# Heads of the first two layers taken two at a time in six visits of a group, and the modulation tiles of both layers dealt out anew

## What is computed

```python
def hybrid_layer(x, c, cos, sin, pre_g, post_g, w_ada, b_ada, w_in, w_out):
    mod = jnp.einsum('bd,de->be', jax.nn.silu(c), w_ada) + b_ada
    shift, scale, gate = jnp.split(mod, 3, axis=-1)
    h = rms_norm(x, pre_g) * (1 + scale[:, None, :]) + shift[:, None, :]
    proj = jnp.einsum('bsd,de->bse', h, w_in)
    qa, ka, va, ga, qb, kb, vb, gb = jnp.split(proj, SPLIT_POINTS, axis=-1)
    ...
    o_a = merge(dilated_mixture_attention(qa, ka, heads(va, N_HEADS_A))) * jax.nn.silu(ga)
    o_b = merge(moba_attention(qb, kb, heads(vb, N_HEADS_B))) * jax.nn.silu(gb)
    y = jnp.einsum('bse,ed->bsd', jnp.concatenate([o_a, o_b], axis=-1), w_out)
    y = rms_norm(y, post_g)
    return x + gate[:, None, :] * y
...
mod = (silu_c @ w_mod[l] + b_mod[l]).reshape(B, 3 * N_SUB, 1, D)
h = rms_norm_2(x, norm_g[l, 1]) * (1.0 + sc) + sh
```

## Time and profile before

| | |
|---|---|
| runs | 1634.32 to 1634.64 us, median 1634.32 us |
| profiled execution | 1635.31 us, of which the span is 1633.5 us |
| granted TensorE clock | 0.999 of full speed |
| busy | PE 98%, DVE 72%, ACT 47%, POOL 4% |

### The profile page before, as it was taken

One profiled execution on the slowest core, in us unless ns is written; L12 is line 12 of the kernel. 1 busy time (PEld: TensorE's weight loads), 2 busy tenths in 40 slices (PEclk: granted clock), 3 DMA queues, 4 the chain that ended last, 5 costly groups with the idle time before them and its releaser, 6 DMA issues.

```text
span 1633.5 us, 20618 instructions
## 1 busy us (share of the span) xinstructions
PE 1607.6 (98%) x7958; PEld 1325.4 (81%) x7958; DVE 1173.3 (72%) x1921; ACT 774.3 (47%) x1221; POOL 63.0 (4%) x95
## 2 busy tenths in 40 slices
PE   6999999999999999999999999999999999999998
PEld 5778777888888888887776888888888888888886
DVE  7778898748976666477645789867877758666654
ACT  4766565542221223254445555535554563554552
POOL 0000100010000000020001100001000100010000
PEclk9999999999999999999999999999999999999999
DMA  9866676325666665242122387866777585455551
GB/s 378 334 246 232 259 269 210 130 99 195 219 217 215 222 226 199 90 160 77 65 88 84 135 329 290 316 232 259 258 282 273 181 329 214 163 192 192 182 183 37
DMA packets 93187, 337.49 MB, mean 207 GB/s; under 512 B 10641, under 2 KB 11281, under 8 KB 92833
## 3 DMA queue, kind: packets, MB, share of 16 engines
q1 hardware_dynamic: 90848, 328.11, 56.1%
q0 software_dynamic: 2240, 8.06, 1.5%
HBM read 335.08 MB, written 1.05 MB: 206 GB/s over the span
## 4 chain that ended last, share of the span: by engine, by line
PE 54%; DVE 2%; issue 1%; ACT 0%; POOL 0%; DVEq 0%; POOLq 0%; ACTq 0%
PE bank L292 52%; PE bank L295 2%; DVE sb_tm L301 0%; DVE sb_XN L309 0%; ACT sb_arena L298 0%; ACT sb_XN L298 0%; DVE sb_X L301 0%; DVE sb_XN L301 0%; DVE sb_sg L316 0%; DVE sb_arena L319 0%; DVE sb_XC L301 0%; DVE sb_w8r L301 0%; DVE sb_w5r L301 0%; POOL sb_rstd L301 0%; DVE sb_arena L312 0%
## 5 line engine op out<-in xcount | busy, mean ns | idle before, releaser
L298 ACT ACTIVATE sb_hi<-sb_w 128x1024 fp32r<-128x1024 f32 x428 | 431.4, 1052 | 289.1 <-DMA sb_w<-in_w 242.3
L292 PE MATMUL bank<-sb_hT,sb_hi 128*128 128x512 f32 x1600 | 527.6, 394 | 0.0
L292 PE MATMUL bank<-sb_hi,sb_hT 128*128 128x512 f32 x1280 | 418.6, 398 | 3.8 <-ACT sb_hT L298 3.3
L292 PEld LDWEIGHTS bank<-sb_hT,sb_hi 128*128 128x128 f32 x1600 | 292.3, 188 | 58.4
L292 PEld LDWEIGHTS bank<-sb_hi,sb_hT 128*128 128x128 f32 x1280 | 241.2, 189 | 60.4 <-issue 7.7
L312 DVE CUSTOM_DVE_ANT_0 sb_w<-sb_w,sb_cb 128x1024 f32<-128x1024 f32 x144 | 174.7, 1218 | 0.0
L301 DVE TENSOR_TENSOR sb_sg<-bank,sb_sg 128x512 f32<-128x512 f32 (+1 forms) x90 | 58.9, 660 | 102.5 <-ACT sb_sg L298 80.7
L298 ACT ACTIVATE sb_sg<-bank 128x512 f32<-128x512 f32 (+1 forms) x98 | 54.9, 574 | 126.5 <-PE bank L292 122.7
L298 ACT ACTIVATE sb_arena<-bank 128x512 f32<-128x512 f32 (+1 forms) x108 | 58.2, 561 | 74.4 <-PE bank L295 38.8
L292 PE MATMUL bank<-sb_arena 128*128 128x64 f32 (+5 forms) x400 | 87.7, 345 | 0.5 <-DVE sb_arena L319 0.5
L301 DVE TENSOR_TENSOR sb_tm<-bank,sb_rows 128x512 f32<-128x512 f32 x40 | 27.6, 691 | 72.4 <-PE bank L292 69.6
(11 more groups left out here) (470 smaller groups left out, 3204.3 us busy)
## 6 DMA issues: line engine op xcount, KB each, us to landing
sb_w<-in_w SPq DMA_DIRECT2D x428, 512.0 KB, 4.2
sb_w<-in_mw SPq DMA_DIRECT2D x192, 512.0 KB, 4.6
sb_rows<-in_na_rpb POOLq DMA_DIRECT2D x16, 96.0 KB, 2.3
sb_X<-in_x SPq DMA_DIRECT2D x1, 1024.0 KB, 4.9
sb_cb<-in_cvec POOLq DMA_DIRECT2D x2, 512.0 KB, 6.9
sb_XC<-in_ctx POOLq DMA_DIRECT2D x1, 1024.0 KB, 9.7
sb_arena<-in_sg_ln_g POOLq DMA_DIRECT2D x1, 1024.0 KB, 6.2
sb_arena<-in_sg_ln_b POOLq DMA_DIRECT2D x1, 1024.0 KB, 9.5
```

Of the source, the lines that this page charges most:

```text
L292: return self.e.matmul(out, a, b, start=start, stop=stop)
L298: return self.e.activation(out, a, f, **kw)
```

## The change

Three edits. (1) A group is worked on in six visits v = 0 to 5 in place of eleven. Visit v of PE holds, in this order: the transposes of head 2v-2, the value products of heads 2v-4 and 2v-3, the scores of heads 2v and 2v+1, the transposes of head 2v-1. ACT copies and exponentiates in turn for both heads, DVE masks both heads, and divides in visits 3 and 5. The visits of group A now stand after units 15, 17, 19, 21, 23, 24 of layer 1 and 10, 12, 14, 16, 18, 19 of layer 2; those of B after 24, 26, 28, 30, 32, 33 and 22, 24, 26, 28, 30, 31. (2) Of the 48 modulation tiles 16 to 63, thirty instead of twenty-four are worked on after units 16 to 34, and eighteen between units 43 and 70 instead of twenty-four between 40 and 66. (3) The squares of the context rows on ACT stand after units 4 to 7 of layer 2 instead of 11 to 14.

```diff
-    for first, last, count in ((16, 34, 24), (40, 66, 24), (W_F00 + 8, W_MX - 10, 64), (W_F01 + 4, W_F10 - 10, 32),
+    for first, last, count in ((16, 34, 30), (43, 70, 18), (W_F00 + 8, W_MX - 10, 64), (W_F01 + 4, W_F10 - 10, 32),
...
-        for i in range(11):
-            B1[0].setdefault(15 + i, []).append(("A", i))
-            B1[0].setdefault(23 + i, []).insert(i < 3, ("B", i))
-            B1[1].setdefault(10 + i, []).append(("A", i))
-            B1[1].setdefault(22 + i, []).insert(0, ("B", i))
+        for v in range(6):
+            B1[0].setdefault((15, 17, 19, 21, 23, 24)[v], []).append(("A", v))
+            B1[0].setdefault((24, 26, 28, 30, 32, 33)[v], []).insert(v == 0, ("B", v))
+            B1[1].setdefault((10, 12, 14, 16, 18, 19)[v], []).append(("A", v))
+            B1[1].setdefault((22, 24, 26, 28, 30, 31)[v], []).insert(0, ("B", v))
...
+        def pe_attention(e, l, g, v):
+            if 1 <= v <= 4:
+                pe_turn(e, l, g, 2 * v - 2)
+            if v >= 2:
+                pe_weigh(e, l, g, 2 * v - 4)
+                pe_weigh(e, l, g, 2 * v - 3)
+            if v < 4:
+                pe_score(e, l, g, 2 * v)
+                pe_score(e, l, g, 2 * v + 1)
+            if 1 <= v <= 4:
+                pe_turn(e, l, g, 2 * v - 1)
...
+        def act_attention(e, l, g, v):
+            for x in range(2):
+                if 1 <= v <= 4:
+                    act_weights(e, l, g, 2 * v - 2 + x)
+                if v < 4:
+                    act_exp(e, l, g, 2 * v + x)
...
+        def dve_attention(e, l, g, v):
+            if v < 4:
+                dve_scores(e, l, g, 2 * v)
+                dve_scores(e, l, g, 2 * v + 1)
+            if v in (3, 5):
+                dve_weighed(e, l, g, v // 4)
...
-                if 11 <= u < 15 and l == 1:
-                    square(e, "cx0", XC, u % 2, (u - 11) // 2, SQ, [done(LD["xc"], 0), *rows_turned("a1")])
+                if 4 <= u < 8 and l == 1:
+                    square(e, "cx0", XC, u % 2, (u - 4) // 2, SQ, [done(LD["xc"], 0), *rows_turned("a1")])
```

More of the change, by code:

```diff
@@ new lines, in pe_score @@
+        def pe_score(e, l, g, h):
+            pr, po = h // 2, 64 * (h % 2)
+            b = BANK["S", l, g, h] = HB3.take()
+            for f in b.free() + heads_ready(l, g, "q") + heads_ready(l, g, "k"):
+                e.wait_ge(*f)
+            q, k = qT[g], kT[g]
+            e.mm(b.ap[:, 0:128], q[po:po + 64, pr, 0:128], k[po:po + 64, pr, 0:128], True, True)
+            e.mm(b.ap[:, 128:384], q[po:po + 64, pr, 128:256], k[po:po + 64, pr, :], True, True).then_inc(
+                SCO.sem, SCO.put(l, g, h))
+            b.till = ((SMX, l, g, h),)
@@ new lines, in pe_turn, with pe_weigh @@
+        def pe_turn(e, l, g, h):
+            b = BANK["P", l, g, h] = HB3.take()
+            for f in b.free():
+                e.wait_ge(*f)
+            e.wait_ge(*done(EX, l, g, h))
+            for x in range(3):
+                m = e.tr(b.ap[:, x * 128:(x + 1) * 128], PB[h % 3][:, x * 128:(x + 1) * 128], ident)
+            m.then_inc(TRP.sem, TRP.put("P", l, g, h))
+            b.till = ((AE, "PT", l, g, h),)
+        def pe_weigh(e, l, g, h):
+            b = bank[7]
+            if h % 4 == 0:
@@ L1008, in pe_attention @@
                 for f in b.free():
                     e.wait_ge(*f)
[L1010 to L1046, removed]
@@ new lines, in pe_weigh @@
+            e.wait_ge(*done(AE, "PT", l, g, h))
+            for j in range(2):
+                e.wait_ge(*done(AE, "p", l, "v", g, j))
+            v, pt, c, o = vv[g], PT[h % 3], slice(h * 64, h * 64 + 64), h % 4 * 64
+            e.mm(b.ap[:, o:o + 64], pt[:, 0:128], v[:, 0, c], True, True)
+            e.mm(b.ap[:, 256 + o:320 + o], pt[:, 128:256], v[:, 0, c], True, False)
+            e.mm(b.ap[:, 256 + o:320 + o], pt[:, 256:384], v[:, 1, c], False, True).then_inc(PVS.sem, PVS.put(l, g, h))
@@ new lines, in pe_weigh, with act_weights @@
+            b.till = ((DE, "O", l, g, h // 4),)
+        def act_attention(e, l, g, v):
[4 more added lines that the diff above has]
+                    act_exp(e, l, g, 2 * v + x)
+        def act_weights(e, l, g, h):
+            e.wait_ge(*done(TRP, "P", l, g, h))
+            if h >= 3:
+                e.wait_ge(*done(PVS, l, g, h - 3))
+            elif g:
+                e.wait_ge(*done(PVS, l, 0, (6, 7, 5)[h]))
+            e.act(PT[h % 3], BANK["P", l, g, h].ap[:, 0:384], ACT.Copy).then_inc(AE.sem, AE.put("PT", l, g, h))
@@ new lines, in dve_weighed @@
+        def dve_weighed(e, l, g, q):
+            r = stat[:, l, g, q * 4:q * 4 + 4, 2:4]
+            e.wait_ge(*done(EX, l, g, q * 4 + 3))
+            e.recip(r, r).then_inc(DE.sem, DE.put("recip", l, g, q))
+            e.wait_ge(DE, DE.n)
+            e.wait_ge(*done(PVS, l, g, q * 4 + 3))
+            if l:
+                for f in squares_done("cx0"):
+                    e.wait_ge(*f)
+            c = slice(g * 512 + q * 256, g * 512 + q * 256 + 256)
+            e.tt(y[:, :, c].rearrange("p j (h d) -> p j h d", d=64),
+                 bank[7].ap[:, :].rearrange("p (j h d) -> p j h d", j=2, h=4),
+                 r.rearrange("p h j -> p j h").unsqueeze(3).to_broadcast([128, 2, 4, 64]), ALU.mult).then_inc(
+                     DE.sem, DE.put("O", l, g, q))
```

61 lines of the change are left out of this document (19 added, 42 removed).

## The result

The changed kernel takes 1619.9 us (median of 4 runs, 1619.5 to 1620.3), the kernel before 1634.5 (4 runs, 1634.3 to 1634.6): a ratio of 0.991, 95% interval 0.9898 to 0.9921, or 14.6 us less. The forecast was 6.3 us less, and the range ended at 1624.0. Direction and place were right, the size was not. (The profiled execution of the kernel before was 0.8 us above its median, so the spans of the two profiles differ by more, 15.4 us.)

The account below looks back on a forecast made before the run. PE, busy 1607.6 of 1633.5 us, was taken as the bound; 6.0 + 0.4 + 0.2 - 0.3 = 6.3 us less gave 1629.0 profiled, 1628.0 as median, range 1624.0 to 1631.5.

Parts of the forecast that it names:

- the price of the second score head: PE's double visits: the odd head's scores cost 0.11 + 0.11 + 0.22 + 0.22 us instead of 0.85; 6.0 us saved.
- Price (c): PE's score pairs: the odd head also overlaps the even head's last 256-column instruction; 13.7 us a group, 9.4 saved.
- The three prices: PE's score pairs: array drains every head, drain saved, or last instruction also overlapped; 3.0, 6.0 or 9.4 us saved.
- rival 1: PE's score pairs: heads overlap in the array at price (c); 9.7 us less, 1624.6 us; chance 0.30.
- price (b): PE's score pairs: no row change or unhidden load between two 64-row heads; 14.6 us a group, 6.0 saved; chance 0.40.
- Tiles in layer 1: Six more modulation tiles on DVE, units 16 to 34: a late tile delays the y transposes 0.3 us, bounds 0 and 2.
- DVE's cover: Last division of group B, layer 1: DVE comes 0.5 us late against a cover of 0.94, so no cost.
- The waits at 198 and 159.86 us: PE's waits in early layer 2 and late layer 1 go with the new tile times: 0.4 and 0.2 us gained.
- Squares: Context-row squares, four at some 0.8 us, moved into ACT's waits at 188 to 200 us of layer 2: cost nothing.
- Rival 3: Visits 1 to 3: three-bank ring makes the last transposes wait for ACT's copy; 4.5 us slower, 1638.8; chance 0.05.
- The lead persists: After layer 2 the same units start earlier by the same amount up to the end, else the forecast fails.

Follow-up runs that it names:

- same rows: The changed kernel with heads taken in the order 0, 2, 1, 3, 4, 6, 5, 7, so both of a pair lie in the same 64 rows: 1627.7 us.
- unstalled run: The changed kernel with the Silu of the condition rows in unit 14, not 20, and layer 2's first y transposes in unit 30, not 29: 1626.1 us.
- paired neighbourhood attention: The changed kernel with the neighbourhood attention's scores of an even and an odd head also issued next to each other: 1618.4 us.
- scores issued ahead: The paired neighbourhood attention with each pair of scores issued at the end of the odd item before, except items 12 and 13: 1620.6 us.
- old tiles: The changed kernel with the modulation tiles at their old times (24 and 24), pairs and moved squares kept: 1622.0 us.

## Why the prediction failed, point by point

- **The step that failed is the price of the second score head.** "The second head costs 0.11 + 0.11 + 0.22 + 0.22 instead of 0.85" is exactly what it costs in the same 64 rows (same rows: 0.65, a full visit 4.06). In the other 64 rows it costs 0.01 (a full visit 3.41). Price (c) let only the even head's last instruction overlap, since I thought of the overlap as something between neighbours in the queue; in fact the two chains of four run side by side. The three prices left out the one that held, 0.01, though the rule of rival 1 leads to it if every instruction is given its partner. 16 pairs x 0.64 = 10.3 us is the missing term. The rest of the forecast stood: in the same rows, where price (b) is paid, the changed kernel is 6.8 us faster than the kernel before, where 6.3 was forecast.
- **The rule of the Trainium skill** that matmuls in different row groups run at the same time ("TensorE: Matmul & The Clock Gate", Part 3, Packing small matmuls) is what the trace now shows, at 13 ns from start to start where it gives about 4 (7 ns at 512 columns); I gave the rule 0.30 and priced it at a third of what it does, and "By that, (c) holds" was my misreading: if every instruction runs beside its partner, the whole odd head goes. The argument against it (float32 scores take two instructions with a load each) counted for nothing.
- **Tiles in layer 1**, +0.3 us ahead of the `y` transposes: right in place and size (0.2, at 147 us), as was DVE's cover. Alone, in eleven visits, the wait can be 1.25 us, inside the bounds of 0 and 2, and for the reason given: the tile of unit 32 lands late.
- **The waits at 198 and 159.86 us** (0.4 and 0.2) are gone as forecast with the pairs; in eleven visits the same tile times removed them too, and other waits cost more. With the pairs the tile times are worth 2.1 us, not 0.6: the stretch of 185 to 205 us was read as it was, and not as it would be once PE comes to it 8 us earlier, where DVE is the late one at 221 us. Squares: nothing, right within the 0.36 us of one wait.
- **Rival 3** (the ring of three banks) was real but small: two of twelve places, 0.45 and 0.49 us, each with ACT late (at 93 us behind 2.0 us of Silu, at 122 behind a table load of 1.28 and a rounding). New waits came to 2.3 us, where 0.3 was taken. Against the ledger: 17.3 us less on PE (7.0 that also come in same rows, 10.3 by the overlap), 2.3 of new waits, 0.6 of old ones gone, so 15.6 over the two layers; unit 80 starts 15.5 us earlier, and the span fell by 15.4. Of the 7.0, 6.0 were forecast; the full visit agrees to 0.01 us, so the missing 1.0 lies in the other visits, and which of them was not traced.
- **The lead persists**: the unit starts are 15.4 to 15.6 us earlier from layer 2's end to the last one, as written.

## What to carry to other kernels

Where a kernel has matmuls of 64 rows, look for a partner in the other 64 rows and issue the two next to each other: in float32 the second was free here, at 128, 256 and 512 columns, and that was 10.3 us of PE's stream. Then count what the followers need: the exponential, the copy and the bank have the same time as before but half the distance on PE, and an engine that takes its work in order must have the piece that PE needs next ahead of the piece that waits for PE. When a price is bounded by the nearest rows, ask what mechanism would make it zero, and keep zero in the range if no row excludes it.

## What was not expected of the hardware

- Two float32 chains in the two halves of the rows run entirely beside each other: starts 13 ns apart for each of four instructions, 0.86 us for both against 0.85 for one; at 512 columns 1.05 us for both against 2.1 for two. In the same half they take 0.65 us more, with no change of rows between them.
- A short idle time of PE can cost more than itself. After 4.6 us of waiting in the unstalled run the clock stood at 0.50 (1.2 of 2.4 GHz) for some 3 us; in the paired neighbourhood attention waits of 1.9 to 4.4 us together stand just before, or at the start of, stretches of some 3 to 13 us at 0.50, while waits of 0.6 us by themselves left it at 1.00. The length of the wait alone does not decide it: behind a single wait of 2.3 us (scores issued ahead) the clock was low for 7 us, behind one of 1.9 us (old tiles) it stayed full:
```profile
857.00:864.00 7.00, 7.00 (x28) 5.38 (x28) 4.46 (x14) 2.66 (x6) 1.20 (x3) 0.51 0.00 0
```
```profile
223.00:226.00 3.00, 2.40 (x22) 2.43 (x23) 2.83 (x6) 1.61 (x4) 0.00 (x0) 1.00 0.66 262
```
